# A feed-forward part in one program, setup parameters issued by ScalarE, and memory rows loaded a stage earlier

## The reference, cut to what matters

```python
def _conv_ffn(h, w_up, conv_w, conv_b, w_down):      # FFN_DIM = 2816, kernel width 3
    u = _dwconv(h @ w_up, conv_w, conv_b)
    gate, val = jnp.split(u, 2, axis=-1)
    return (jax.nn.gelu(gate, approximate=True) * val) @ w_down

# in each layer i
    f = _conv_ffn(_rmsnorm(x, norm_g[i, 2]), ffn_w_up[i], ffn_conv_w[i], ffn_conv_b[i], ffn_w_down[i])
    x = x + _rmsnorm(f, norm_g[i, 3])
# in the second block, memory_attention begins with
    kv = jnp.einsum('bmd,dc->bmc', rmsnorm(mem, g_mem), w_mem_kv)    # mem: 256 rows of 1024
```

## Time and profile before

| | us |
|---|---|
| median of 3 executions (2811.98 to 2815.3) | 2812.07 |
| the profiled execution, its time | 2814.07 |
| the profiled execution, its span | 2812.2 |
| PE busy in it | 2481.3 |
| mean granted TensorE clock, as a share of full speed | 0.939 |

### The profile page before, as it was taken

One profiled execution on the slowest core, in us unless ns is written; L12 is line 12 of the kernel. 1 busy time (PEld: TensorE's weight loads), 2 busy tenths in 40 slices (PEclk: granted clock), 3 DMA queues, 4 the chain that ended last, 5 costly groups with the idle time before them and its releaser, 6 DMA issues. The chain is left out here.

```text
span 2812.2 us, 33931 instructions
## 1 busy us (share of the span) xinstructions
PE 2481.3 (88%) x12483; PEld 2031.4 (72%) x12483; DVE 1490.0 (53%) x2238; ACT 1030.3 (37%) x1718; POOL 234.3 (8%) x264
## 2 busy tenths in 40 slices
PE   5999996688999897998899989799697888599995
PEld 4777785576888785766688877587486677599994
DVE  4766445544555434744555544367897574433333
ACT  3423332334454335423445433433323533133332
POOL 0000001100000000000000000455141000010111
PEclk9999998889999998999999999899897999699997
DMA  4122232122332421112233322223021021699995
GB/s 140 68 83 90 90 105 75 48 88 60 95 100 82 155 80 61 62 59 75 75 97 97 119 105 75 77 89 111 30 74 47 24 90 46 231 373 368 373 377 208
DMA packets 212860, 330.59 MB, mean 118 GB/s; under 512 B 13861, under 2 KB 109997, under 8 KB 212749
## 3 DMA queue, kind: packets, MB, share of 16 engines
q1 hardware_dynamic: 208013, 312.33, 32.4%
q0 software_dynamic: 4736, 16.78, 2.0%
HBM read 299.99 MB, written 29.10 MB: 117 GB/s over the span
## 5 line engine op out<-in xcount | busy, mean ns | idle before, releaser
L366 PE MATMUL ps<-ffn_h_hi,ffn_w_hi 128*128 128x512 f32 x704 | 275.6, 391 | 10.5 <-DVE ffn_h_lo L361 10.5
L367 PE MATMUL ps<-ffn_h_lo,ffn_w_hi 128*128 128x512 f32 x704 | 275.3, 391 | 0.0
L368 PE MATMUL ps<-ffn_h_hi,ffn_w_lo 128*128 128x512 f32 x704 | 275.0, 391 | 0.0
L366 PE MATMUL ps<-wo_hi,lhs_hi 128*128 128x512 f32 x608 | 242.4, 399 | 34.0 <-DVE lhs_lo L361 34.0
L3912 PEld LDWEIGHTS ps<-expert_x,ring 128*128 128x128 f32 x2048 | 235.8, 193 | 8.1 <-DVE expert_x L3995 3.4
L367 PE MATMUL ps<-wo_lo,lhs_hi 128*128 128x512 f32 x608 | 240.8, 396 | 0.0
L368 PE MATMUL ps<-wo_hi,lhs_lo 128*128 128x512 f32 x608 | 240.7, 396 | 0.0
L3912 PE MATMUL ps<-expert_x,ring 128*128 128x96 f32 x2048 | 235.6, 276 | 3.8 <-DVE expert_x L3995 3.0
L361 POOL TENSOR_TENSOR w_lo<-ring,w_hi 128x512 fp32r<-128x512 f32 (+1 forms) x112 | 160.5, 1434 | 750.9 <-ACT w_hi L518 750.2
L361 DVE TENSOR_TENSOR wo_lo<-ring,wo_hi 128x1024 fp32r<-128x1024 f32 x76 | 93.0, 1223 | 185.5 <-ACT wo_hi L653 185.5
L2245 DVE SCALAR_TENSOR_TENSOR y_tmp<-ps,pcol,y_tmp 128x511 f32<-128x511 f32 x88 | 61.9, 745 | 219.8 <-ACT y_tmp L2217 219.8
(11 more groups left out here) (625 smaller groups left out, 5220.9 us busy)
## 6 DMA issues: line engine op xcount, KB each, us to landing
ring<-in_w_up SPq DMA_DIRECT2D x32, 2048.0 KB, 11.1
ring<-in_ffn_w_up SPq DMA_DIRECT2D x88, 512.0 KB, 4.9
moe_down<-in_w_down SPq DMA_DIRECT2D x32, 1024.0 KB
ring<-in_ab_w_in SPq DMA_DIRECT2D x13, 2048.0 KB, 7.9
ring<-in_w_in SPq DMA_DIRECT2D x11, 2048.0 KB, 7.7
ring<-in_ffn_w_down SPq DMA_DIRECT2D x10, 2048.0 KB, 7.7
ring<-in_c_w_in SPq DMA_DIRECT2D x6, 2048.0 KB, 7.9
expert_results<-expert_y SPq DMA_DIRECT2D x32, 384.0 KB, 7.4
```

The lines of the kernel that those rows point to most:

```text
L366: nc.tensor.matmul(out, left[0], right[0], start=start, stop=False, **more)
L367: nc.tensor.matmul(out, left[0], right[1], start=False, stop=False, **more)
L368: return nc.tensor.matmul(out, left[1], right[0], start=False, stop=stop, **more)
```

## The change

Three things are changed. Setup: ACT issues the 35 small transfers ahead of its root, and SP issues x, the first chunk and the slices, waits for the parameters, and issues the second chunk. Feed-forward: `ffn_up` and `ffn` become one function with one program. All parts lie in one buffer, `area`, of 16 x 1024 columns; the five held down rows take over places of the up weights and of the up inputs, so ACT's split of row n waits for the products that read them. Row 0's pieces are made in the last turn's first half, those of rows 1 and 2 in its second, and PE takes row 0 before the last taps have read banks 2 and 3: tiles 2, 3 and 0 first, then tile 1 behind `va`. The gain rows are issued at the start of the program, and down chunk 0 is asked for after 42 remainders instead of 44. Memory rows: they are loaded at the end of layer 1's feed-forward program, behind the second turned tile, into the first two tiles of `y_tmp`; their own buffer and program go, and the scratch of their norm moves to the other two tiles.

```diff
@@ def setup
             sp.dma_start(k.x[:, :, :], A["x"].rearrange("o (t p) d -> p (o t) d", p=P)).then_inc(k.weights_loaded.sem, 16)
-            for g, r, ap in plan:
-                sp.dma_start(rows[r:r + ap.shape[0], g, :], ap).then_inc(k.param_loaded.sem, 16)
-            for dst, src in bplan:
-                sp.dma_start(dst, src).then_inc(k.param_loaded.sem, 16)
             load_weights(k, sp, first[0])
             for dst, src in extra:
                 sp.dma_start(dst, src).then_inc(extra_loaded.sem, 16)
+            sp.wait_ge(*k.param_loaded(16 * (len(plan) + len(bplan))))
             load_weights(k, sp, first[1])
-            sp.wait_ge(*k.param_loaded(16 * (len(plan) + len(bplan))))
...
         def _(act):
+            for g, r, ap in plan:
+                nc.scalar.dma_start(rows[r:r + ap.shape[0], g, :], ap).then_inc(k.param_loaded.sem, 16)
+            for dst, src in bplan:
+                nc.scalar.dma_start(dst, src).then_inc(k.param_loaded.sem, 16)
             norm_root(k, act, NT)
@@ def norm_to_cm
+            if loaded is not None:
+                dve.wait_ge(*loaded(16))
@@ def ffn (new, from ffn_up)
+ROWS_AHEAD = 1
+    def down_parts(n):
+        at = [0, 4 * D, 7 * D, 10 * D, 13 * D][n % ROWS_HELD]
+        rows, left = area[:, at:at + 2 * D], area[:, at + 2 * D:at + 3 * D]
+        return [rows[:, 0:D], rows[:, D:2 * D]], [left[:, 0:T], left[:, T:2 * T]]
...
         @block.sync
         def _(sp):
+            sp.dma_start(gnext[:, :], everywhere(next_gain, D)).then_inc(k.param_loaded.sem, 16)
+            sp.dma_start(k.gpost[:, :], everywhere(gain, D)).then_inc(k.param_loaded.sem, 16)
             with sp.Fori(1, TURNS) as i:
...
-            sp.wait_ge(*k.w_lo_ready(2 * FT))
-            for chunk in down:
-                load_weights(k, sp, chunk)
+            for c in range(len(chunks)):
+                sp.wait_ge(*k.w_lo_ready(2 * FT - 2 if c == 0 else 2 * FT + 4 * (c - 1) if c >= 2 else 2 * FT))
+                load_weights(k, sp, chunks[c])
+            for nxt in after:
+                sp.wait_ge(*k.w_lo_ready(3 * FT))
...
             with pe.Fori(1, TURNS) as i:
                 turn(i)
+            for n in range(ROWS_AHEAD):
+                pe.wait_ge(*k.w_lo_ready(2 * FT + n + 1))
+                pe.wait_ge(*k.h_lo_ready(KD + n + 1))
+                for t in (2, 3):
+                    tile(n, t)
+                if n == 0:
+                    pe.wait_ge(*k.va(FT - 1))
+                tile(n, 0)
+            pe.wait_ge(*k.va(FT))
+            for n in range(ROWS_AHEAD):
+                tile(n, 1).then_inc(k.products.sem, 1)
+            for n in range(ROWS_AHEAD, FT):
+                pe.wait_ge(*k.w_lo_ready(2 * FT + n + 1))
+                pe.wait_ge(*k.h_lo_ready(KD + n + 1))
...
@@ ACT: finish, with the down rows between the next turn's split and gelu
                 if ahead:
                     split(i + 1, s)
+                for n in down:
+                    split_down(n)
                 wait(act, k.va, i, 2, s + 1)
...
+            def split_down(n):
+                if n % 4 == 0:
+                    act.wait_ge(k.loaded[landed[n // 4][0]].sem, landed[n // 4][1])
+                act.wait_ge(*k.products(FT - 1 if n == 0 else FT if n < ROWS_HELD else FT + n - ROWS_HELD + 1))
+                act.wait_ge(*k.vb(2 + n + 1))
+                rows, left = down_parts(n)
+                nc.scalar.copy(rows[0], down_raw(n)).then_inc(k.w_hi_ready.sem, 1)
+                nc.scalar.copy(left[0], g_cm[:, n, :]).then_inc(k.h_hi_ready.sem, 1)
...
-            for s in range(2):
-                finish(TURNS - 1, s, False)
+            finish(TURNS - 1, 0, False, range(ROWS_AHEAD))
+            finish(TURNS - 1, 1, False, range(ROWS_AHEAD, ROWS_AHEAD + 2))
+            for n in range(ROWS_AHEAD + 2, FT):
+                split_down(n)
+            steps(result, norm, read_out)
@@ DVE: finish
                 if ahead:
                     remainders(i + 1, s)
+                for n in down:
+                    down_remainders(n)
                 wait(dve, k.sb, i, 2, s + 1)
...
@@ removed: def ffn, with its project_out(k, lambda n: g_cm[:, n, :], ...)
@@ block 2
+def memory_rows(k):
+    return k.ytmp[:, 0:MT, :]
+    def load(sp):
+        sp.wait_ge(*k.acc_ready(MT))
+        sp.dma_start(memory_rows(k), k.A["mem_2"].rearrange("o (t p) d -> p (o t) d", p=P)).then_inc(k.memory_loaded.sem, 16)
...
-            mem = sb("mem_tm", [P, MT, D], to=e)
-            with nc.Block(no_gpsimd_drain=True) as block:
-                @block.sync
-                def _(sp):
-                    sp.dma_start(mem[:, :, :], A["mem_2"].rearrange("o (t p) d -> p (o t) d", p=P)).then_inc(k.param_loaded.sem, 16)
-                    sp.wait_ge(*k.param_loaded(16))
-            norm_to_cm(k, mem, k.pcol[:, 5, 32:40], mcm, k.ytmp, tiles=MT)
+            norm_to_cm(k, memory_rows(k), k.pcol[:, 5, 32:40], mcm, k.ytmp[:, MT:2 * MT, :], tiles=MT, loaded=k.memory_loaded)
...
-        ffn(k, 1, A["norm_g"][1, 3], A["g_mix_2"][0], memory_weights(k))
+        ffn(k, 1, A["norm_g"][1, 3], A["g_mix_2"][0], memory_weights(k) + [load_memory_rows(k)])
```

More of the change, by code:

```diff
@@ L2150, in ffn_first, with ffn @@
     return load
-def ffn_up(k, layer, h_hi, h_lo, g_cm, ybuf, w_hi, w_lo, down):
+ROWS_AHEAD = 1
+def ffn(k, layer, gain, next_gain, after):
     nc = k.nc
@@ L2161, in ffn_up @@
     tap2, bias = k.pcol[:, 2 + 2 * layer, 0:2 * FT], k.pcol[:, 2 + 2 * layer, 2 * FT:4 * FT]
+    chunks = out_chunks(k.A["ffn_w_down"][layer], FT)
+    ss, root, ss2, root2 = (k.stat[:, n, 0:NT] for n in range(4))
+    bulk = FT - KEPT
+    scratch = k.ytmp
+    landed = []
+    for _ in chunks:
+        s = sum(k.taken) % 2
+        k.taken[s] += 1
+        landed.append((s, 16 * k.taken[s]))
     def column(cols, i, s, half):
@@ L2197, in turn, with tile, turned @@
                                 pe.wait_ge(*k.h_lo_ready(c + 1))
-                            last = product(nc, bank(s, half), [part[:, s, half, c, :] for part in (w_hi, w_lo)], [h[:, c, :] for h in (h_hi, h_lo)],
+                            last = product(nc, bank(s, half), [up_part(which, s, half)[:, c, :] for which in range(2)], [h[:, c, :] for h in (h_hi, h_lo)],
                                            c == 0, c == KD - 1)
                     last.then_inc(k.products.sem, 1)
+            def tile(n, t):
+                rows, left = down_parts(n)
+                for half in range(2):
+                    last = product(nc, k.ps[:, 2 * t + half, :], [x[:, t * P:(t + 1) * P] for x in left], [x[:, half * BANK:(half + 1) * BANK] for x in rows],
+                                   n == 0, n == FT - 1, skip_group_check=True)
+                return last
+            def turned(t):
+                pe.wait_ge(*k.norm_ready(t + 1))
+                for c in range(KD):
+                    last = nc.tensor.transpose(k.ps[:, 2 * t + c // NT, (c % NT) * P:(c % NT + 1) * P], scratch[:, t, c * P:(c + 1) * P], k.ident[:, :])
+                last.then_inc(k.acc_ready.sem, 1)
             turn(0)
@@ L2204, in _ @@
                 turn(i)
+            for n in range(ROWS_AHEAD):
[12 more added lines that the diff above has]
+                pe.wait_ge(*k.h_lo_ready(KD + n + 1))
+                if n < bulk:
+                    for t in range(NT):
+                        last = tile(n, t)
+                    last.then_inc(k.products.sem, 1)
+            for t in range(NT):
+                if t == NT - 1:
+                    turned(0)
+                for n in range(bulk, FT):
+                    last = tile(n, t)
+                last.then_inc(k.products.sem, 1)
+            for t in range(1, NT):
+                turned(t)
         @block.scalar
@@ L2211, in split, with finish @@
                 for half in range(2):
-                    nc.scalar.copy(w_hi[:, s, half, :, :], up_slot(k, s)[:, :, half, :]).then_inc(k.w_hi_ready.sem, 1)
-            def finish(i, s, ahead):
+                    nc.scalar.copy(up_part(0, s, half), up_slot(k, s)[:, :, half, :]).then_inc(k.w_hi_ready.sem, 1)
+            def finish(i, s, ahead, down=()):
                 wait(act, k.products, i, 2, s + 1)
@@ L2270, in _ @@
                     finish(i, s, True)
-            for s in range(2):
-                finish(TURNS - 1, s, False)
-    for signal in (k.products, k.sa, k.sb, k.va):
+            finish(TURNS - 1, 0, False, range(ROWS_AHEAD))
+            finish(TURNS - 1, 1, False, range(ROWS_AHEAD, ROWS_AHEAD + 2))
+            for n in range(ROWS_AHEAD + 2, FT):
+                down_remainders(n)
+            dve.wait_ge(*k.param_loaded(32))
+            steps(result, norm, read_out)
+    for signal in (k.sa, k.sb, k.va):
         signal.close(FT)
+    k.products.close(FT + bulk + NT)
     k.vb.close(FT + 2)
[L2276 to L2279, removed]
+    k.h_hi_ready.close(KD + FT)
+    k.h_lo_ready.close(KD + FT)
+    k.w_hi_ready.close(3 * FT)
+    k.w_lo_ready.close(3 * FT)
```

(3 more changed lines are left out.)

77 lines of the change are left out of this document (72 added, 5 removed).

## The result

| | before | after |
|---|---|---|
| median | 2813.69 (2811.98 to 2815.58, 4 executions) | 2784.07 (2778.14 to 2784.66, 4 executions) |
| ratio | | 0.989, 95% interval 0.9873 to 0.9907 |
| the profiled execution, its time | 2814.07 | 2778.14 |
| its span | 2812.2 | 2776.1 |
| its mean granted clock | 0.939 | 0.946 |

Faster by 29.6 in the median, which is 5.1 above the 2779.0 forecast and inside 2773 to 2790. The profiled execution is the fastest of its four. Lines of `setup` have moved by 1 to 3; the feed-forward helper's casts are now L2330 and L2331, its taps L2381 and L2385.

What follows compares the result with a forecast made beforehand. PE is busy for 88% of the span, so time is won only where it idles or runs at its lower clock. -22.0 - 5.5 - 5.6 = -33.1 on 2814.07 gives 2781.0, as median 2779.0 us; range 2773 to 2790.

Steps and rivals of the forecast that it cites:

- A, the seams: Feed-forward seam, two layers: stretch from last up product to row 1 shrinks from 17.6 to 6.6, clock staying up; -22.0.
- B, the memory rows: End of layer 1's feed-forward program: memory rows load earlier, so DVE starts on them where SP did; -5.5.
- The cover of 4: Memory rows: they are there at 1758 and the program lasts until 1762, leaving 4 to spare.
- C, the setup: Setup: ACT issues the 35 small transfers, so the setup's end goes from 26.1 to about 20.5; -5.6.
- The correction of 2.0 from execution to median: Total time: the median shown is 2.0 below the profiled execution, so 2781.0 becomes 2779.0.
- Two issuers, one at a time: Setup: issues of SP and ACT exclude each other, so the gain there is only -1.5 and the time 2783; chance 0.15.
- The seam stays cold: Feed-forward seams: the clock falls as before, 2.8 a layer given back, time 2784.6; chance 0.09.
- Pieces late: Feed-forward seams: chunk 0 or DVE's part of row 1 comes late, each seam loses 1 to 3, 2781 to 2785; chance 0.06.
- Slower: Setup: ACT's issue of a small transfer is dear, 2.2 each, setup ends near 82.5, time 2841; chance 0.02.

Runs made afterwards that it cites:

- `undo_setup`: Kernel after with the small transfers back on SP and the wait at the end, as in the kernel before; median 2783.8 us.
- `setup_shared`: Kernel after with the 12 broadcasts moved to SP between first chunk and slices, the 23 rows staying on ACT; median 2778.89 us.
- `again`: Kernel after, run again with no edit; median 2777.35 us.
- `setup_first`: Kernel after with the 12 broadcasts on SP ahead of the first chunk, rows on ACT, slices behind the parameter wait; median 2785.0 us.
- `row0_late`: Kernel after, but PE waits for the last taps before its first tile of row 0; median 2796.11 us.

## Why the prediction was right, and where it was off

**A, the seams (−22.0).** Right in its steps: no wait for row 0's pieces, a gap of 0.39 at the taps (0.5 was said), one of 0.36 at row 1 (0.6), row 1 at 6.6 after the last up product (6.6), the clock at 1.00 in both. Measured −10.85 twice, −21.7. The 8.2 of idle and 2.8 of clock could not be run apart from each other. What no term held is the gated attention behind layer 0's part, 2.8 quicker along with the seam. The gain rows cost nothing that the trace shows.

**B, the memory rows (−5.5).** Measured −5.4 at the place, 5.3 by the run that undoes it. The cover of 4 held.

**C, the setup (−5.6).** Measured −4.8. The steps on ACT came as said (35 issues done at 15.53 for 14.7, the table load behind them, DVE's end at 20.1 for 19.3). The mis-sized term is the landing of the last parameter: 2.1 by the earlier trace rows, a median over two 32 KB transfers elsewhere in the kernel, but 4.9 here, behind 34 others of its kind. (By the prediction's own terms the landing comes at 14.7 + 2.1 = 16.8; it said 18, as if counted from behind the table load, so the term was short by 2.8, more than the 18 lets see.) That put the second chunk's issue at 20.48 instead of 18, and so SP, done at 20.85, and not DVE, done at 20.09, became the last: 0.8, the whole error. The other difference cancelled: DVE was 0.8 later than said, but the next program follows the last engine by 0.5 (20.85 to 21.37, in `undo_setup` 25.47 to 26.04), where I had left 1.2 behind DVE. `setup_shared`, which shortens DVE's chain by 2.8, gained only 1.5, since the landing held it.

**The sum.** −31.9 against −33.1 at the places. The profiled execution is lower than 2781.0 by 2.9, since stages without an edit gave 4.2 where the places gave 1.2 less than said. The median is higher than 2779.0 by 5.1; the places do not explain it, for they keep their distances in every trace that has them, and the executions behind the median were not traced. So the places are right by their mechanism, and that the total lies within 5.1 of the forecast is in part luck; the median of `again` lies 1.6 below it. The correction of 2.0 from execution to median had the right sign for before and the wrong one for after, whose profiled execution was its fastest (median 5.9 above it).

**The rivals.** *Two issuers, one at a time*: refuted. ACT's issues keep 0.32 to 0.45 while SP stands 9.90 in its slices, and in `setup_first` 25 issues whose lengths add up to 9.5 on one engine are out in 6.0 on two. The rule of the Trainium skill (Perfetto Trace Analysis, section DMA Instruction — HWDGE) that the descriptor generator is locked "for exclusive use" may hold for a part of an issue, which no row resolves; it does not hold for the whole length that the trace shows as an issue. *The seam stays cold*: it did not, with gaps of 0.39 and 0.36; `row0_late` shows that its mechanism exists one step away, at 4.46 idle. *Pieces late*: no, row 0's went ahead without a wait. *Slower*: ACT's dearest issue of a small transfer was 0.45, not 2.2; in `setup_first`, with another order, one cost 1.89, so the mechanism exists.

## What to carry to other kernels

Where one stage's last outputs must pass three engines before the next stage can start, look for work of the next stage that needs none of them: three tiles of 1.36 hid a chain of 4.5 and, by keeping the idle time to 0.39, kept the clock. Read what a part brings as the jump at its place in two aligned traces, since here two medians of one and the same program lay 6.7 apart. Look behind the place too: a stage 120 later was quicker by 2.8 whenever the seam had no long wait. And do not read an issue's length as work where something large is outstanding: two slices cost 0.99, 3.15, 6.24 or 9.90 in four orders.

## What the runs showed of the hardware that was not expected

- The length of an issue in the trace includes waiting for room, on small transfers too: a 16 KB broadcast took 3.81 on SP behind x and a chunk, against 0.36 in `undo_setup`, while ACT's issues in its own queue went on at 0.32 to 0.59. The other queue is not always spared: in `setup_first` ACT's issues cost up to 1.89.
- With the 12 broadcasts ahead of the chunk on SP the first transposes came at 25.07 (`setup_first`), with them behind it at 19.89 (`setup_shared`). The slices stood in different places too, but moving them alone changed 21.37 to 21.48. Ahead of the chunk the small transfers ran at 36 to 68 GB/s while it waited; that this is the reason is argued, not tested.
- A wait of 4.46 in the seam lowered the granted clock to 0.50, waits of 0.39 and 0.36 did not, and a stage 120 later was slower by 2.8 to 4.9 in the three traces that had a wait of 4.46 or 9.20.
- One kernel's executions differ by 7 (2775.7 to 2783.01 in `again`), and two traces of it by up to 5 in between, while the gaps in the touched places stay the same within 0.1. In both traces the steps lie where PE's granted clock changes level: from 2120 to 2215 the kernel after spends three stretches at 0.50, `again` one.
